# Gate weights' low half, table of further blocks and weight loads reordered at the entry into the experts of a hybrid decoder layer

## The chip, the core and the metric

The kernel runs on one core of a Trainium2 chip, in one launch. The metric is device time in microseconds. A core has five engines with queues of their own: PE (matmul; PEld is its weight load), DVE (vector), ACT (scalar), POOL (which here issues gathers and scatters) and SP (which here only issues loads). Sixteen DMA engines move the data for all of them.

## What is computed

One decoder layer over 1024 prompt tokens and 32 sample tokens, width 1024: an input projection, a convolution branch and a gated linear attention branch, an output projection, then a two-level mixture of experts, then a norm. The change lies where the experts begin.

```
g_idx  = argmax(softmax(x @ w_rg + b_rg))           # one of 4 groups
top_i  = top_k(e_logits of that group, 2)           # two of its 8 experts
# pairs (token, expert) sorted by expert, padded to blocks of 128 rows
xb = xt[row_tok].reshape(n_blocks, 128, D_MODEL)    # gather
hidden = silu(xblk @ w_g[e]) * (xblk @ w_u[e])      # 1024 -> 512
yb = hidden @ w_d[e]                                # 512 -> 1024
y = segment_sum(yb * row_wt, row_tok)               # scatter with add
```

## The kernel before

Tokens go through the layer in nine tiles of 128 (the last has 32). For each tile DVE picks group and experts and counts the rank of every pair inside its expert (`place`), then makes the pair's weight (`weigh`). Every expert has one block of 128 rows (blocks 0 to 31). Pairs beyond the 128th of an expert go to further blocks, at most 16, whose number is found at run time; in this run the trace shows 36 blocks in all. `lst_tok` (in the trace `kdT`) holds the tokens of each block, `lst_w` their weights. Both come out of bank 7, where PE adds one-hot products tile by tile; `list_last` adds the last tile, and DVE then copies the bank.

A block `n` is worked as follows, with two buffers for everything that has the index `n % 2`:

- SP loads three weight matrices of 2 MB each (`load_w`, L504: gate, up, down) into `wraw`, each when PE is done with the block before last in that buffer.
- POOL gathers the block's 128 token rows (`gather`, L988, `stage` in the trace, 4 KB a row).
- PE transposes them (`x_block`, L1524). ACT rounds them and the weights to a high half (`xeH`, `wH_`); DVE makes the low half, the rest (`x_low`, `weight_low`: `xeL`, `wL_`). A product is then three matmuls: high by high, high by low, low by high.
- PE does the gate product (24 matmuls of 512 columns), transposes the rows of block `n + 1`, does the up product (24) and the down product of block `n - 1` (24).
- POOL scatters the result with add into `h_scr` (`scatter`, L997), each scatter after the one before it has landed.

Every engine works through its own list in the order in which the code issues it; semaphores tie the lists together. `keep_running(n)` (L1107) is `n` matmuls of ones by the identity whose result nobody reads: it only keeps PE busy. Each of them shows in the trace as two records.

The steps at the entry, before the change, with their lines: DVE `weigh(8)` (L2613 to L2618), copy of the counts (L2740) and of `lst_w` (L2742), low half of the gate weights, `x_low(0)`, low half of the up weights, then the table of further blocks (L2749 to L2767, a dozen small operations on 16 partitions, which ends in `more_made`), then block 0. POOL: `gather(0)`, `gather(1)`, the last slots, `gather(2)`, then it waits for `more_made`, stores the table, gathers the further blocks' lists (`qe`), and goes on with `gather(3)`. SP: after `gather(0)` has landed, down weights of block 0, up weights of block 1, down weights of block 1.

## Time and profile before

| | us |
|---|---|
| time, median of 3 runs (1714.29 to 1717.73) | 1715.81 |
| the profiled execution's own time | 1714.82 |
| its span | 1713.0 |
| PE busy in the span | 1665.4 (97%) |
| DVE busy | 1264.9 (74%) |
| ACT busy | 930.4 (54%) |
| POOL busy | 248.8 (15%) |

The entry into the experts lies at about 1025 to 1050 us of the span, and the experts fill the time from there to about 1675 us. A busy share is a mean over stages with different limits, and a busy PE is not a PE at its peak. The profiled execution is one of many: its own time is 0.99 us under the median of the three.

### The profile page before, as it was taken

What the parts mean: (1) busy time and instruction counts of PE and PEld (TensorE: products, weight loads), DVE (VectorE), ACT (ScalarE), POOL (GpSimd) and SP (SyncE); (2) the same over time, 40 slices, a digit from 0 to 9 for tenths busy, and PEclk for the clock granted to TensorE, in tenths of its full rate; (3) what the DMA queues carried; (4) which work ended last, traced back from release to release, by engine and by line L of the source; (5) the groups of instructions that cost most, each with busy time, mean ns of one, the idle gap of its engine ahead of it and who ended that gap; (6) DMA issues with size and microseconds to landing.
All of it is one profiled execution on the core that took longest, in us unless ns stands there. A gap on an engine that the chain in (4) does not pass through costs nothing.

```text
span 1713.0 us, 24990 instructions
## 1 busy us (share of the span) xinstructions
PE 1665.4 (97%) x9010; PEld 1463.1 (85%) x9010; DVE 1264.9 (74%) x2101; ACT 930.4 (54%) x1184; POOL 248.8 (15%) x269
## 2 busy tenths in 40 slices
PE   8999999999999999999999999999999999999994
PEld 7999987777999999879998888888888888888882
DVE  5234799986766667655464558999889899889886
ACT  6363121216433344426343337887878778788785
POOL 4100111110000000011001123511111212122111
PEclk9999999999999999999999998999999999999998
DMA  5402223231243233366343339999999999999975
GB/s 203 145 26 75 75 100 107 94 108 57 93 142 105 93 93 93 102 199 214 117 166 129 105 105 373 390 394 380 383 378 384 377 382 371 377 381 381 384 276 221
DMA packets 103171, 367.26 MB, mean 214 GB/s; under 512 B 14628, under 2 KB 58872, under 8 KB 88240
## 3 DMA queue, kind: packets, MB, share of 16 engines
q1 hardware_dynamic: 79824, 308.76, 48.2%
q0 software_dynamic: 23056, 57.36, 10.3%
q8 instruction: 47, 0.77, 0.2%
q14 instruction: 36, 0.29, 0.1%
q10 hardware_dynamic: 208, 0.08, 0.0%
HBM read 326.24 MB, written 61.22 MB: 226 GB/s over the span
## 4 chain that ended last, share of the span: by engine, by line
PE 72%; PEld 15%; DMA 4%; DVE 3%; ACT 2%; issue 2%; DVEq 1%; SPq 0%; ACTq 0%; PEldq 0%; POOLq 0%
PE bank L1069 68%; PEld bank L1069 15%; PE bank L1524 2%; DMA wraw_down<-in_w_expert_down 1%; DMA wraw_up<-in_w_expert_up 1%; PE bank L1548 1%; DMA uo<-in_x_prompt 1%; DVE gwork L2107 1%; PE bank L1441 0%; DMA h_scr<-ybuf,kdT 0%; ACT L1641 0%; PEld bank L1288 0%; DMA s<-in_state_gla 0%; DMA wraw_gate<-h_scr 0%; DVE wraw_gate L2674 0%
## 5 line engine op out<-in xcount | busy, mean ns | idle before, releaser
L2107 DVE TENSOR_TENSOR wL_down<-wraw_down,wH_down 128x1024 fp32r<-128x1024 f32 x140 | 162.0, 1218 | 25.6 <-ACT wH_down L1641 25.1
L2107 DVE TENSOR_TENSOR wL_up<-wraw_up,wH_up 128x2048 fp32r<-128x2048 f32 x72 | 161.6, 2285 | 21.6 <-ACT wH_up L1641 21.6
L2107 DVE TENSOR_TENSOR wL_gate<-wraw_gate,wH_gate 128x2048 fp32r<-128x2048 f32 x72 | 161.7, 2287 | 12.1 <-ACT wH_gate L1641 12.1
L1641 ACT ACTIVATE wH_up<-wraw_up 128x2048 fp32r<-128x2048 f32 x72 | 134.0, 1909 | 66.2 <-DMA wraw_up<-in_w_expert_up 51.8
L2232 DVE SCALAR_TENSOR_TENSOR ybuf<-uo,gwork,ybuf 128x1024 f32<-128x1024 f32 x120 | 154.5, 1288 | 6.1 <-issue 6.1
L1641 ACT ACTIVATE wH_down<-wraw_down 128x1024 fp32r<-128x1024 f32 x140 | 136.6, 1051 | 18.5 <-DMA wraw_down<-in_w_expert_down 18.4
L1641 ACT ACTIVATE stage<-bank 128x512 f32<-128x512 f32 (+3 forms) x65 | 34.5, 546 | 190.2 <-PE bank L1069 180.8
L997 POOL DMA_INDIRECT h_scr<-ybuf,kdT x34 | 77.1, 2269 | 399.7 <-ACT ybuf L1641 360.9
L1641 ACT ACTIVATE wH_gate<-wraw_gate 128x2048 fp32r<-128x2048 f32 x72 | 134.5, 1934 | 1.2 <-DMA wraw_gate<-in_w_expert_gate 1.2
L1069 PE MATMUL bank<-nTH,gateH 128*128 128x352 f32 x384 | 129.5, 337 | 0.7 <-issue 0.6
L1069 PE MATMUL bank<-nTH,slabH 128*128 128x352 f32 x384 | 124.9, 325 | 1.2 <-ACT uo L1641 0.7
L1069 PE MATMUL bank<-nTH,gateL 128*128 128x352 f32 x384 | 124.0, 323 | 0.0
L1069 PE MATMUL bank<-nTL,gateH 128*128 128x352 f32 x384 | 123.5, 322 | 0.0
L1069 PE MATMUL bank<-nTH,slabL 128*128 128x352 f32 x384 | 123.2, 321 | 0.0
L1069 PE MATMUL bank<-nTL,slabH 128*128 128x352 f32 x384 | 123.1, 321 | 0.0
L1069 PE MATMUL bank<-wH_up,xeH 128*128 128x512 f32 x288 | 115.9, 403 | 0.0
L1069 PE MATMUL bank<-wH_gate,xeH 128*128 128x512 f32 x296 | 115.4, 390 | 0.0
L1069 PE MATMUL bank<-wH_gate,xeL 128*128 128x512 f32 x296 | 115.3, 390 | 0.0
L1069 PE MATMUL bank<-wH_up,xeL 128*128 128x512 f32 x288 | 112.7, 391 | 0.0
L1069 PE MATMUL bank<-wL_up,xeH 128*128 128x512 f32 x288 | 112.2, 390 | 0.0
L1069 PE MATMUL bank<-wL_gate,xeH 128*128 128x512 f32 x288 | 112.0, 389 | 0.0
L1069 PE MATMUL bank<-wH_down,hidTH 128*128 128x512 f32 x280 | 109.5, 391 | 1.2 <-DVE hidTL L2107 1.2
(359 smaller groups left out, 4279.5 us busy)
## 6 DMA issues: line engine op xcount, KB each, us to landing
wraw_gate<-in_w_expert_gate SPq DMA_DIRECT2D x36, 2048.0 KB, 19.1
wraw_up<-in_w_expert_up SPq DMA_DIRECT2D x36, 2048.0 KB
wraw_down<-in_w_expert_down SPq DMA_DIRECT2D x36, 2048.0 KB
slab_raw<-in_w_in SPq DMA_DIRECT2D x7, 2048.0 KB, 9.6
gate_scr<-stage POOLq DMA_DIRECT2D x16, 528.0 KB, 3.6
vr_scr<-stage POOLq DMA_DIRECT2D x32, 256.0 KB, 2.3
gate_raw<-in_w_in SPq DMA_DIRECT2D x16, 512.0 KB, 8.7
vrbuf<-vr_scr SPq DMA_DIRECT2D x16, 512.0 KB, 6.9
```

What stands on the lines that cost most here:

```text
L997: pool.indirect_dma_start(out=h_scr, in_=yo[n % 2], in_offset=None, out_offset=bass.IndirectOffsetOnAxis(ap=lst_tok[:, n:n + 1], axis=0), ...
L1069: return pe.matmul(out, lhsT=lhsT, rhs=rhs, start=start, stop=stop, **kw)
L1524: last = pe.transpose(bk[k // 4][:, P * (k % 4):P * (k % 4 + 1)], xg[b][:, k:D:KC], ident[:, :])
L1548: last = pe.transpose(bk[4][:, P * k:P * (k + 1)], hid[:, k:DE:FC], ident[:, :])
L1641: return act.activation(out, in_, func, **kw)
L2107: return dve.tensor_tensor(out, x, y, op)
L2232: dve.scalar_tensor_tensor(ybuf[:, c, 0:SEQ], u[:, c, bass.ds(w, SEQ)], tap, ybuf[:, c, 0:SEQ], ALU.mult, ALU.add)
```

## The change

On DVE, the gate weights' low half, `x_low(0)` and the up weights' low half come directly behind `weigh(8)`; the copies of the counts and of `lst_w` come after them, and the table of further blocks after block 2. On PE, four `keep_running` matmuls move from behind to ahead of the last list product of the tokens; sixteen instead of two stand ahead of `x_block(0)`; the last list product of the weights and the sum of the counts come behind it, and two instead of eight `keep_running` matmuls ahead of the first gate product. On POOL, `gather(3)`, `gather(4)` and `scatter(0)` come ahead of the wait for the table. On SP, the weight loads wait for `gather(0)` and `gather(1)`, and the up weights of block 1 come ahead of the down weights of block 0. The steps that follow the table move two blocks later, and PE and DVE run blocks 3, 4 and 5 written out, with the loop from block 6.

```diff
@@ SP
             sp.wait_ge(xg_loaded[0], 16)
+            sp.wait_ge(xg_loaded[1], 16)
+            load_w(sp, W_UP, 1, 1)
             load_w(sp, W_DOWN, 0, 0)
-            load_w(sp, W_UP, 1, 1)
             sp.wait_ge(hn_made, NT)
@@ POOL
             gather(2)
+            gather(3)
+            gather(4)
+            scatter(0)
             pool.wait_ge(more_made, 1)
...
-            for n in range(NE - 3):
+            for n in range(2, NE - 3):
                 gather(n + 3)
-                if n >= 1:
-                    scatter(n - 1)
+                scatter(n - 1)
@@ PE
             ranks(NT - 1)
+            keep_running(4, bk[3])
             pe.wait_ge(slot_made, 2 * NT - 1)
             list_last(tok_hot, 0).then_inc(tok_listed, 1)
-            keep_running(4, bk[3])
-            pe.wait_ge(w_hot_made, NT)
-            list_last(w_hot, NE).then_inc(w_listed, 1)
-            mm(bk[5][:, 0:NE], ones[:, 0:P], macc[:, :], True, True).then_inc(count_ready, 1)
...
             pe.wait_ge(lists_ready, 1)
+            keep_running(16, bk[3])
+            x_block(0, 16)
+            pe.wait_ge(w_hot_made, NT)
+            list_last(w_hot, NE).then_inc(w_listed, 1)
+            mm(bk[5][:, 0:NE], ones[:, 0:P], macc[:, :], True, True).then_inc(count_ready, 1)
             keep_running(2, bk[3])
-            x_block(0, 16)
-            keep_running(8, bk[3])
             block_products(0, 0, 16, None, first=True)
             block_products(1, 1, 32, None)
             block_products(2, 0, 32, None)
+            block_products(3, 1, 48, None)
+            block_products(4, 0, 48, None)
             pe.wait_ge(lists_f, 1)
...
-            block_products(3, 1, 48, None)
-            with pe.Fori(2, NE // 2 - 1) as i:
+            block_products(5, 1, 64, None)
+            with pe.Fori(3, NE // 2 - 1) as i:
@@ DVE
+            weight_low(W_GATE, 0, 0)
+            x_low(0, 0)
+            weight_low(W_UP, 0, 0)
             dve.wait_ge(count_ready, 1)
             dve.tensor_copy(cnt, bk[5][:, 0:NE])
             dve.wait_ge(w_listed, NT)
             dve.tensor_copy(by_turn(lst_w), in_turns(bk[7][:, NE:2 * NE]))
             dve.drain()
-            weight_low(W_GATE, 0, 0)
-            x_low(0, 0)
-            weight_low(W_UP, 0, 0)
+            dve_block(0, 0, True, None, first=True)
+            dve_block(1, 1, True, None)
+            dve_block(2, 0, True, None)
+
             dve.wait_ge(const_ready, 7)
...
             dve.tensor_copy(m_int, m_out).then_inc(more_made, 1)
-            dve_block(0, 0, True, None, first=True)
-            dve_block(1, 1, True, None)
+            dve_block(3, 1, True, None)
             dve.wait_ge(listed_rows, 16)
```

PE's list between the last rank product and the first gate product. In it `kdn,state` and `macc,ones` 32x32 are the rank product, `ebuf,kdT` a list product, `ident,ones` the `keep_running` matmuls, `ident,stage` the transposes of `x_block(0)`. Before:

```order
L1069 MATMUL bank<-kdn,state 32x32
L1069 MATMUL bank<-macc,ones 32x32
L1069 MATMUL bank<-ebuf,kdT 128x32 x2
L1069 MATMUL bank<-ident,ones 128x128 x4
L1069 MATMUL bank<-ebuf,kdT 128x32 x2
L1069 MATMUL bank<-macc,ones 128x32
L1069 MATMUL bank<-ident,ones 128x128 x2
L1524 MATMUL bank<-ident,stage 128x128 x8
L1069 MATMUL bank<-ident,ones 128x128 x8
L1069 MATMUL bank<-wH_gate,xeH 128x512
```

And now:

```order
L1072 MATMUL bank<-kdn,state 32x32
L1072 MATMUL bank<-macc,ones 32x32
L1072 MATMUL bank<-ident,ones 128x128 x4
L1072 MATMUL bank<-ebuf,kdT 128x32 x2
L1072 MATMUL bank<-ident,ones 128x128 x16
L1524 MATMUL bank<-ident,stage 128x128 x8
L1072 MATMUL bank<-ebuf,kdT 128x32 x2
L1072 MATMUL bank<-macc,ones 128x32
L1072 MATMUL bank<-ident,ones 128x128 x2
L1072 MATMUL bank<-wH_gate,xeH 128x512
```

The second list product and the sum of the counts have gone behind the transposes, and most of the idle matmuls ahead of them.

DVE's list from the end of `weigh(8)` (`ebuf<-kdn,pay`). `small<-bank` is the copy of the counts, `kdT<-bank` that of `lst_w`, `qe<-small,mtab` the first operation of the table. Before:

```order
L2618 TENSOR_SCALAR ebuf<-kdn,pay 32x32 x2
L2740 COPY small<-bank 128x32
L2742 COPY kdT<-bank 128x32
L2107 TENSOR_TENSOR wL_gate<-wraw_gate,wH_gate 128x2048 x2
L2107 TENSOR_TENSOR xeL<-bank,xeH 128x512 x2
L2107 TENSOR_TENSOR wL_up<-wraw_up,wH_up 128x2048 x2
L2107 TENSOR_TENSOR qe<-small,mtab 16x256
```

And now:

```order
L2623 TENSOR_SCALAR ebuf<-kdn,pay 32x32 x2
L2112 TENSOR_TENSOR wL_gate<-wraw_gate,wH_gate 128x2048 x2
L2112 TENSOR_TENSOR xeL<-bank,xeH 128x512 x2
L2112 TENSOR_TENSOR wL_up<-wraw_up,wH_up 128x2048 x2
L2748 COPY small<-bank 128x32
L2750 COPY kdT<-bank 128x32
L2112 TENSOR_TENSOR xeL<-bank,xeH 128x512 x2
```

The two copies stand behind the weights now, and block 0 (its `xeL` is the last row) follows without the table. The table now stands between the down weights of block 2 and the low half of its hidden rows.

POOL's list from the last slots of tile 7 (`slot_scr`) on. `stage` is a gather, `h_scr<-ybuf` a scatter, the three rows from `IOTA` on are what waits for the table. Before:

```order
L960 DMA slot_scr<-pay,small 36864x2 x4
L988 DMA stage<-xn_scr,kdT 128x1024 x2
L960 DMA slot_scr<-pay,small 36864x2 x2
L988 DMA stage<-xn_scr,kdT 128x1024
L1028 IOTA attn 128x32
L1030 DMA more_scr<-small 16x4
L1032 DMA qe<-slot_scr,small 16x256
L988 DMA stage<-xn_scr,kdT 128x1024 x2
L997 DMA h_scr<-ybuf,kdT 1056x1024
L988 DMA stage<-xn_scr,kdT 128x1024
```

And now:

```order
L961 DMA slot_scr<-pay,small 36864x2 x4
L989 DMA stage<-xn_scr,kdT 128x1024 x2
L961 DMA slot_scr<-pay,small 36864x2 x2
L989 DMA stage<-xn_scr,kdT 128x1024 x3
L998 DMA h_scr<-ybuf,kdT 1056x1024
L1032 IOTA attn 128x32
L1034 DMA more_scr<-small 16x4
L1036 DMA qe<-slot_scr,small 16x256
L989 DMA stage<-xn_scr,kdT 128x1024
L998 DMA h_scr<-ybuf,kdT 1056x1024
```

The gather behind the three rows was that of block 3 and is now that of block 5.

## Rows read from the trace of the kernel before

**Rows 1.** The page, part 2: DMA share in 40 slices of the span

```profile
DMA  5402223231243233366343339999999999999975
```

**Rows 2.** Stretches: length; PE, PEld, DVE, ACT, POOL busy; PE clock, DMA share, GB/s

```profile
1123.72:1141.47 17.75, 17.75 (x86) 14.90 (x85) 15.92 (x13) 14.45 (x15) 2.61 (x2) 1.00 1.02 404
1602.84:1620.59 17.75, 17.11 (x81) 14.06 (x80) 14.28 (x13) 14.03 (x15) 3.64 (x2) 1.00 1.01 390
```

**Rows 3.** Chain of waits by time (start us, us, what), 1095 to 1665

```profile
1114.74 0.90 PE bank L1524 x8
...
1132.49 0.90 PE bank L1524 x8
...
1588.01 23.36 DMA wraw_down<-in_w_expert_down
...
1636.74 22.68 DMA wraw_up<-in_w_expert_up
```

**Rows 4.** Gate loads, issue to landing, 1060 to 1110, then 1450 to 1640

```profile
DMA to landing us min/median/max: 11.4/11.4/11.4
...
DMA to landing us min/median/max: 21.3/22.3/24.3
```

**Rows 5.** Timeline of PE at the entry (start us, us, what)

```profile
1032.68 1.05 PE L1069 MATMUL bank<-ebuf,kdT 32*128 32x32 f32 x4 [1.64 <-DVEq L2608]
1033.66 2.08 PE L1069 MATMUL bank<-ident,ones 128*128 128x128 f32 x8
1038.21 1.97 PE L1524 MATMUL bank<-ident,stage 128*128 128x128 f32 x8
1039.97 3.21 PE L1069 MATMUL bank<-ident,ones 128*128 128x128 f32 x16
1042.93 0.48 PE L1069 MATMUL bank<-wH_gate,xeH 128*128 128x512 f32 x1
```

**Rows 6.** The same timeline, idle matmuls and a list product ten microseconds earlier

```profile
1021.99 2.03 PE L1069 MATMUL bank<-ident,ones 128*128 128x128 f32 x16
1027.21 0.66 PE L1069 MATMUL bank<-ebuf,kdT 128*128 128x64 f32 x4
```

**Rows 7.** Busy time in the two microseconds in which the granted clock changes

```profile
1032.00:1033.00 1.00, 0.32 (x2) 0.32 (x2) 0.70 (x5) 1.00 (x1) 0.00 (x0) 0.68 0.97 411
1042.00:1043.00 1.00, 1.00 (x9) 1.00 (x8) 1.00 (x3) 1.00 (x2) 1.00 (x1) 0.70 1.02 426
```

**Rows 8.** Timeline of DVE at the entry and in block 2, then one of ACT

```profile
1035.18 0.38 DVE L2618 TENSOR_SCALAR ebuf<-kdn,pay 32x32 f32<-32x32 f32 x2
1037.69 4.49 DVE L2107 TENSOR_TENSOR wL_gate<-wraw_gate,wH_gate 128x2048 fp32r<-128x2048 f32 x2
1042.10 1.28 DVE L2107 TENSOR_TENSOR xeL<-bank,xeH 128x512 fp32r<-128x512 f32 x2
1047.70 0.41 DVE L2107 TENSOR_TENSOR qe<-small,mtab 16x256 f32<-16x256 f32 x1
1050.99 0.16 DVE L2767 CAST small<-small 16x4 int32<-16x4 f32 x1
1093.42 4.61 DVE L2107 TENSOR_TENSOR wL_down<-wraw_down,wH_down 128x1024 fp32r<-128x1024 f32 x4
...
1039.42 0.60 ACT L1641 ACTIVATE xeH<-bank 128x512 fp32r<-128x512 f32 x1 [6.16 <-PE bank L1524]
```

**Rows 9.** Timeline of POOL at the entry

```profile
1034.88 1.07 POOL L988 DMA_INDIRECT stage<-xn_scr,kdT  x1 [3.95 <-DVE kdT L2637]
1036.25 1.03 POOL L988 DMA_INDIRECT stage<-xn_scr,kdT  x1 [0.30 <-issue]
1053.40 2.04 POOL L988 DMA_INDIRECT stage<-xn_scr,kdT  x1 [0.31 <-issue]
```

**Rows 10.** Gathers, issue to landing, 1045 to 1600; then the one of 1036.25

```profile
DMA to landing us min/median/max: 12.1/13.6/15.5
...
stage<-xn_scr,kdT POOLq DMA_INDIRECT x1, 4.2
```

More of the change, by code:

```diff
@@ L2774, in _ @@
             dve.tensor_copy(mlf[:, :, 1], mli[:, :, 1].bitcast(F32)).then_inc(lists_f, 1)
-            dve_block(2, 0, True, None)
+            dve_block(4, 0, True, None)
             dve.wait_ge(lists_T, 1)
@@ L2779, in _ @@
             dve.drain().then_inc(lists_ready, 1)
-            dve_block(3, 1, True, None)
-            with dve.Fori(2, NE // 2 - 1) as i:
+            dve_block(5, 1, True, None)
+            with dve.Fori(3, NE // 2 - 1) as i:
                 for b in range(2):
```

## The prediction

> **What bounds the kernel now.** I read four views, in this order. First the slices of the page: from the entry into the experts on, the DMA engines are busy in nine tenths or more of nearly every slice [rows 1]. A single block shows both limits side by side: PE busy 17.75 of 17.75 us and a DMA share of 1.02 [rows 2]. The transposes of two blocks follow each other at 1114.74 and 1132.49, so a block takes 17.75 us of PE [rows 3]. Second, the landing times say which of the two really has no room. A gate load takes 11.4 us from issue to landing early on and 22.3 us (21.3 to 24.3) late [rows 4]. The loads are issued by PE's progress, so landings that come ever later behind their issue mean that the DMA engines need a little more than 17.75 us for a block and fall back behind PE: by 22.3 - 11.4 = 10.9 us over some thirty blocks, about 0.36 us each. Third, the end of the chain of waits: it runs through a down load of 23.36 us (1588.01) and an up load of 22.68 us (1636.74) [rows 3], and just there PE is short of its full time for the first time (17.11 of 17.75, DMA share 1.01) [rows 2]. So PE sets the pace for most of the experts, and the DMA engines, which have caught up with its lead by about 1610, set the end. Fourth, the timelines at the entry, for the terms below.
>
> **The gate weights' low half.** DVE is through with `weigh(8)` at 1035.18 + 0.38 = 1035.56 and begins the gate weights at 1037.69 [rows 8], because it waits for a list product and the sum of the counts. It then needs until 1042.10, begins `x_low`, and PE's first gate product starts at 1042.93, 0.83 us behind that [rows 5, 8]. With the weights directly behind `weigh(8)` that is 2.13 us less, perhaps 0.1 of it lost to the handover: 2.0.
>
 The DVE way then gives a first gate product 2.0 + 0.4 = 2.4 us sooner, at 1040.5. The other way to it is the gather: issued at 1034.88, its rows were transposed from 1038.21, 3.33 us later [rows 5, 9]; now 1037.8. The sixteen idle matmuls ahead of it cost 32 records, twice the 2.03 us of 16 at the high clock [rows 6], 4.1 us from about 1033.6: 1037.7, just done. ACT's first half of `xeH` began 1.21 us after the transposes and took 0.60 [rows 5, 8]: 1039.6, no later than DVE's weights at 1039.7. The two list steps behind the transposes and the last two idle matmuls fit before 1040.5. So PE enters the experts 2.4 us sooner; if the clock does fall, see the third rival.
>
> **The wait of the weight loads.** They waited for the landing at 1038.2, at which the transposes start, and now wait for `gather(1)` too, which landed 4.2 us after 1036.25, at 1040.45, with the weights already running beside it [rows 9, 10]. Alone it should need the 3.33 us of the first: 1039.2 after the 0.4 us saved. So the loads start between 1039.2 and 1040.1, 1.0 to 1.9 us later. Against that, half of this gather's half megabyte has no more to be moved then; at the 404 GB/s of rows 2 that is 0.6 us. What the DMA engines begin later they end later, since they are never free again: a shift of 0.4 to 1.3 us, and I take 0.8. The exchange of up and down weights costs nothing: the three loads together are 6 MB, 16 us, and neither is used before PE has done a first up product.
>
> **The table moved.** It takes DVE from 1047.70 to 1050.99 + 0.16 = 1051.15, 3.45 us [rows 8]. It stood in the shadow of the first gate product; behind block 2 it stands in the stretch in which DVE works without a break, with its last down part ending at 1093.42 + 4.61 = 1098.03 [rows 8]. Less the 2.4 us of the entry that is 1095.6, or up to 1.9 later if the gate weights of block 2, the first to land behind the delayed loads, hold ACT up. The hidden rows of block 2 wait behind the table, until 1099.8 to 1101.6 with 0.7 for their own step; PE wants them behind the up product of block 3. The transposes ahead of that product stand a block before the 1114.74 of rows 3, at 1096.99, now 1094.6; they take 0.9, and the product a third of the rest of a block, about 5.5: near 1101.0. Cost: 0, at most 0.6.
>
> **What waits for the table.** This is the larger matter. POOL stands at the wait for `more_made` with `gather(5)` and `scatter(1)` behind it. The table is ready at 1095.6 + 3.45 = 1099.1 to 1101.0. Before, the gather behind it was issued 1053.40 - 1051.15 = 2.25 us after [rows 8, 9]; so `gather(5)` goes out between 1101.3 and 1103.2. Under the load of the weights a gather needs 13.6 us to land (12.1 to 15.5) [rows 10]: 1115.9, with bounds of 1113.4 and 1118.7. PE wants it in block 4, at 1114.74 - 2.4 = 1112.3 [rows 3]. So PE stands for 1.1 to 6.4 us, and I take 3.0, since less is queued ahead of it than late in the run. Nothing gives PE this back, but the DMA engines have 11.4 us of work queued at this time [rows 4], so they do not stand with it. `scatter(1)` is late too; it has until block 3's result is to be put into the same buffer, about 1124, some 20 us.
>
> What the Trainium skill says of this differs. "DMA: Bandwidth & Descriptors", section "Queues, rings and completion order", has each engine take turns between the queues that have work, a packet at a time. By that rule a gather beside the weights should need about twice its own time and not the time of all that is queued, and `gather(5)` would not stand in PE's way. The 12.1 to 15.5 us of rows 10 against 4.2 speak against it; the sum goes by the rows, and what would follow is in the first rival.
>
> **The sum.** On PE's way: -2.4 for the entry, +3.0 for `gather(5)`, 0 for the table: +0.6. On the DMA engines' way: +0.8. The end goes by the later of two ways that lie within a microsecond of each other, and by the end of the chain of waits by that of the DMA engines: +0.8 us. Against the profiled execution's own 1714.82 (span 1713.0 and 1.82 around it) this makes 1715.6; that execution is 0.99 under the median of the runs, so against the median of 1715.81 it is 1716.6.
>
> **Rivals.**
>
> 1. The entry's gain arrives whole. For it: PE is busy 97% of the span and sets each block's pace, and if gathers take turns with weights there is no stand in block 4. Against it: landings of 22 us late in the run [rows 4], and PE's first shortfall beside a DMA share of 1.01 [rows 2]. Time: 1715.8 - 2.4 = 1713.4, and that is still only 0.14%.
>
> 2. Slower: `gather(5)`, held by the table. If it is issued at 1103.2 and lands after 15.5 us, PE stands for 6.4 us; less 2.4 that is +4.0, and 1719.8. This decides when the stand is over 5.8 us, so that PE's way is over 3.4 us longer. For it: POOL's list, in which the gather stands right behind the wait. Against it: it needs late landings on both sides.
>
> 3. The clock falls all the same. Then the 32 idle records ahead of the transposes run at the low clock: eight of them took 2.08 us [rows 5], so 32 take some 8, from 1034 to 1042. From the start of the transposes to the end of ACT's first half 1.8 us passed [rows 5, 8], and from DVE's step to the first product 0.83: 1044.6, which is 1.7 us later than before. `gather(5)` is then wanted 4.1 us later than in the forecast and PE hardly stands for it. PE's way is +1.7 to +2.2. Time: 1715.8 + 1.9 = 1717.7. Against it: the idle matmuls now fill the stretch in which the clock fell.
>
> 4. The loads start 1.9 us late and each delay is kept, while PE stands little: 1717.1. This is the upper end of the forecast and not apart from it.
>
> **How the numbers follow.** Under 0.2%, 3.4 us, a measurement of this kernel cannot tell a change from none. Chances: forecast 0.60, gain kept 0.15, slower by the gather 0.13, clock falls 0.12. Faster by over 0.2% would need more than the whole 2.4 us of the entry: 0.07, most of it measurement. Slower by over 0.2%: most of the second rival and a part of the third: 0.16. Same: 0.77. The range runs from the first rival, 1713.3, to just short of the second, 1719.5.
>
> **What would show it.** After the change: the first gate matmul at 1040.5, with the granted clock at 1.00 throughout from 1030; SP's three loads at 1039.2 to 1040.1; DVE's table near 1096 to 1100; `gather(5)` issued at 1101 to 1103; an idle PE ahead of the transposes of block 5, near 1112; then, at the end, up and down loads of 20 us or more in the chain again, with the last up load landing at 1660 against 1659.4. The prediction is wrong if PE does not stand in block 4, if the last loads land as much earlier as PE is ahead (then the DMA engines did not set the end), or if the loss of the stand is carried to the end in full.

## The result, and the profile after

| | median us | runs |
|---|---|---|
| before | 1714.19 (1712.52 to 1718.98) | 20 |
| after | 1719.13 (1716.52 to 1723.98) | 20 |

The ratio is 1.0026, 95% interval 1.0018 to 1.0034: slower by over 0.2% in the middle of the interval. The profiled execution of the changed kernel took 1719.45 us, its span is 1717.5, against 1714.82 and 1713.0. Line numbers in the changed kernel are up to 5 higher for the helpers (L1072 was L1069, L2112 was L2107).

The page looks almost as it did [rows 1]. Three of the forty slices differ, by one digit each; one of them, lower, is at the entry:

```profile
DMA  5402223241243233356343338999999999999975
```

Two stretches of one block each (length; PE, PEld, DVE, ACT, POOL busy; PE clock, DMA share, GB/s):

```profile
1135.36:1153.11 17.75, 17.75 (x87) 14.90 (x86) 15.69 (x14) 14.44 (x15) 3.96 (x2) 1.00 1.01 385
1596.77:1614.52 17.75, 17.75 (x87) 14.90 (x86) 14.50 (x12) 13.02 (x14) 1.52 (x2) 1.00 1.01 379
```

PE is full in both, but the second is not the late stretch of [rows 2]: it ends where the transposes of block 33 start, and that of [rows 2] goes past them and takes in a wait that comes behind. The stretch from the transposes of block 33 to those of block 34 in the changed kernel, then in the kernel before, and there the one from block 34 to block 35 too:

```profile
1614.48:1635.09 20.61, 18.28 (x87) 14.74 (x86) 17.89 (x14) 17.42 (x17) 5.86 (x3) 1.00 0.96 367
```

```profile
1611.48:1630.15 18.67, 18.03 (x86) 14.81 (x85) 17.17 (x13) 15.83 (x16) 4.54 (x3) 1.00 0.95 358
1630.15:1648.72 18.57, 18.04 (x86) 14.82 (x85) 15.26 (x12) 16.21 (x16) 1.32 (x1) 1.00 0.99 366
```

So in both kernels the blocks take 17.75 us each up to block 33 and longer only at the very end.

**The entry.** PE's timeline, then DVE's, POOL's and SP's (start us, us, what), against [rows 5, 8, 9]:

```profile
1032.87 3.84 PE L1072 MATMUL bank<-ident,ones 128*128 128x128 f32 x32 [0.28 <-DVE kdT L2642]
1037.15 1.16 PE L1524 MATMUL bank<-ident,stage 128*128 128x128 f32 x8 [0.44 <-DMA stage<-xn_scr,kdT]
1039.65 0.50 PE L1072 MATMUL bank<-wH_gate,xeH 128*128 128x512 f32 x1
```

```profile
1034.50 4.49 DVE L2112 TENSOR_TENSOR wL_gate<-wraw_gate,wH_gate 128x2048 fp32r<-128x2048 f32 x2
```

```profile
1035.10 2.59 POOL L989 DMA_INDIRECT stage<-xn_scr,kdT  x1 [0.31 <-issue]
```

```profile
1040.86 0.33 SPq L504 DMA_DIRECT2D wraw_up<-in_w_expert_up  x1
1041.23 0.91 SPq L504 DMA_DIRECT2D wraw_down<-in_w_expert_down  x2
```

The first gate product starts at 1039.65 instead of 1042.93, 3.28 us sooner. The gate weights' low half starts 3.19 us sooner than the 1037.69 of before. The loads start at 1040.86, 2.68 us later than before (1038.18).

**Block 2.** ACT waits for the gate weights, and PE for their low half; three rows of ACT, DVE and PE, in this order:

```profile
1067.07 1.92 ACT L1646 ACTIVATE wH_gate<-wraw_gate 128x2048 fp32r<-128x2048 f32 x1 [5.46 <-DMA wraw_gate<-in_w_expert_gate]
...
1069.02 4.49 DVE L2112 TENSOR_TENSOR wL_gate<-wraw_gate,wH_gate 128x2048 fp32r<-128x2048 f32 x2 [4.35 <-ACT wH_gate L1646]
...
1071.46 0.47 PE L1072 MATMUL bank<-wH_gate,xeH 128*128 128x512 f32 x1 [1.95 <-DVE wL_gate L2112]
```

**The table and `gather(5)`.** DVE, POOL and PE, in this order:

```profile
1098.72 0.41 DVE L2112 TENSOR_TENSOR qe<-small,mtab 16x256 f32<-16x256 f32 x1
...
1102.08 0.67 DVE L2112 TENSOR_TENSOR hidTL<-bank,hidTH 128x512 fp32r<-128x512 f32 x1
```

```profile
1102.24 0.16 POOL L1032 IOTA attn<- 128x32 f32 x1 [22.20 <-DVE small L2776]
...
1104.45 2.62 POOL L989 DMA_INDIRECT stage<-xn_scr,kdT  x1 [0.31 <-issue]
```

```profile
1102.86 0.47 PE L1072 MATMUL bank<-wH_down,hidTH 128*128 128x512 f32 x1 [1.07 <-issue]
...
1116.95 1.16 PE L1524 MATMUL bank<-ident,stage 128*128 128x128 f32 x8 [2.46 <-DMA stage<-xn_scr,kdT]
```

POOL stood for 22.20 us at the table and then issued `gather(5)`. PE stood twice: 1.07 us ahead of the down product of block 2, and 2.46 ahead of the transposes of block 5. The profile puts the first down to "issue". It is the hidden rows' low half, which stood behind the table: DVE ends it at 1102.08 + 0.67 = 1102.75, and PE goes on at 1102.86. A product that needs several things at once can hide its last releaser in this way, and the timeline of the other engine tells it.

The chain of waits, as in [rows 3]: a chain through `gather(5)` first, then one block after the other, then the two loads.

```profile
1104.45 12.46 DMA stage<-xn_scr,kdT
...
1135.48 0.90 PE bank L1524 x8
1136.38 16.38 PE bank L1072 x72
1153.23 0.90 PE bank L1524 x8
...
1591.01 23.40 DMA wraw_down<-in_w_expert_down
...
1641.67 21.34 DMA wraw_up<-in_w_expert_up
```

The transposes give PE's place against before. At the start of block 5 they stand at 1116.95 instead of 1114.6 and from block 6 on 3.0 us behind (1135.36 by PE's timeline, 1132.3 before). They keep this distance for 28 blocks of 17.75 us. The late down load was issued 1591.01 - 1588.01 = 3.0 us later, the last up load landed at 1663.01 instead of 1659.42, 3.6 later, and the span is 4.5 longer. The way there, block by block, in us against before:

| block whose transposes start | 0 | 1 | 2 | 3 | 4 | 5 | 6 to 33 | 34 | 35 | end |
|---|---|---|---|---|---|---|---|---|---|---|
| after | -1.1 | -3.3 | -3.3 | -1.1 | -1.6 | +2.4 | +3.0 | +4.9 | +4.1 | +4.5 |

The gain of 3.3 us is there. 2.2 are lost to the late gate weights, 4.0 in block 4 (1.07 and 2.46 as above, and 0.5 that no wait shows). Two small differences of 0.5 and 0.6 lie where the loop starts, which is two blocks later, and cancel.

### The profile page after: what moved, and what is told of

Read it like the earlier page. It is cut to its first block, busy times and chain, and to the rows that moved or that the text cites. A ratio compares the mean times of both kernels' runs of the same rounds, so it can differ in the third digit from the quotient of the medians.

```text
span 1717.5 us, 24989 instructions
## 1 busy us (share of the span) xinstructions
PE 1667.1 (97%) x9026; PEld 1463.7 (85%) x9026; DVE 1264.8 (74%) x2101; ACT 930.9 (54%) x1184; POOL 236.8 (14%) x269
## 4 chain that ended last, share of the span: by engine, by line
PE 83%; DMA 6%; DVE 3%; issue 3%; ACT 2%; DVEq 1%; SPq 0%; ACTq 0%; POOL 0%; POOLq 0%
PE bank L1072 79%; DMA wraw_up<-in_w_expert_up 2%; PE bank L1524 2%; DMA wraw_down<-in_w_expert_down 1%; DMA stage<-xn_scr,kdT 1%; DMA uo<-in_x_prompt 1%; PE bank L1548 1%; DVE gwork L2112 1%; DMA h_scr<-ybuf,kdT 1%; PE bank L1444 0%; PE bank L1291 0%; ACT L1646 0%; ACT ybuf L1646 0%; DMA wraw_gate<-h_scr 0%; DVE wraw_gate L2679 0%
## 5 line engine op out<-in xcount | busy, mean ns | idle before, releaser
L2112 DVE TENSOR_TENSOR wL_up<-wraw_up,wH_up 128x2048 fp32r<-128x2048 f32 x72 | 161.6, 2285 | 23.7 <-ACT wH_up L1646 23.7
L2112 DVE TENSOR_TENSOR wL_down<-wraw_down,wH_down 128x1024 fp32r<-128x1024 f32 x140 | 162.0, 1219 | 22.7 <-ACT wH_down L1646 22.3
L2112 DVE TENSOR_TENSOR wL_gate<-wraw_gate,wH_gate 128x2048 fp32r<-128x2048 f32 x72 | 161.7, 2287 | 18.6 <-ACT wH_gate L1646 18.5
L1072 PE MATMUL bank<-nTH,gateH 128*128 128x352 f32 x384 | 129.5, 337 | 0.7 <-issue 0.6
L1072 PE MATMUL bank<-nTH,slabH 128*128 128x352 f32 x384 | 124.9, 325 | 1.2 <-ACT uo L1646 0.7
L1072 PE MATMUL bank<-nTH,gateL 128*128 128x352 f32 x384 | 124.0, 323 | 0.0
L1072 PE MATMUL bank<-nTL,gateH 128*128 128x352 f32 x384 | 123.5, 322 | 0.0
L1072 PE MATMUL bank<-nTH,slabL 128*128 128x352 f32 x384 | 123.1, 321 | 0.0
L1072 PE MATMUL bank<-nTL,slabH 128*128 128x352 f32 x384 | 123.1, 321 | 0.0
L998 POOL DMA_INDIRECT h_scr<-ybuf,kdT x34 | 67.3, 1980 | 401.8 <-ACT ybuf L1646 343.1
L1072 PE MATMUL bank<-wH_gate,xeH 128*128 128x512 f32 x296 | 115.5, 390 | 3.6 <-DVE wL_gate L2112 1.9
L1072 PE MATMUL bank<-wH_up,xeH 128*128 128x512 f32 x288 | 115.9, 402 | 0.0
L1072 PE MATMUL bank<-wH_gate,xeL 128*128 128x512 f32 x296 | 115.3, 390 | 0.0
L1072 PE MATMUL bank<-wH_up,xeL 128*128 128x512 f32 x288 | 112.7, 391 | 0.0
L1072 PE MATMUL bank<-wL_up,xeH 128*128 128x512 f32 x288 | 112.2, 390 | 0.0
L1072 PE MATMUL bank<-wL_gate,xeH 128*128 128x512 f32 x288 | 112.1, 389 | 0.0
L1072 PE MATMUL bank<-wH_down,hidTH 128*128 128x512 f32 x280 | 109.3, 391 | 1.7 <-issue 1.1
## 6 DMA issues: line engine op xcount, KB each, us to landing
wraw_down<-in_w_expert_down SPq DMA_DIRECT2D x36, 2048.0 KB, 19.5
```

Source lines behind the costliest of these rows:

```text
L998: pool.indirect_dma_start(out=h_scr, in_=yo[n % 2], in_offset=None, out_offset=bass.IndirectOffsetOnAxis(ap=lst_tok[:, n:n + 1], axis=0), ...
L1072: return pe.matmul(out, lhsT=lhsT, rhs=rhs, start=start, stop=stop, **kw)
L2112: return dve.tensor_tensor(out, x, y, op)
```

## The experiments

There are two theories, D and G where an expectation names them by a letter. D is the prediction's: the DMA engines, which are never free again, set the end, so the start of the loads counts and what PE loses is absorbed. G: PE's own way is carried to the end, and `gather(5)` is what the change costs. In every experiment the profile is one execution, and it lies up to 3.7 us from its kernel's median, so the verdict is the ratio's. It is against runs of before on the same chip. The three columns behind it are of the profiled execution: its own time, the start of the transposes of block 10 against the profile of before, and the span against that of before (1713.0).

| kernel | ratio (95% interval) | median us | profiled us | PE at block 10 | span |
|---|---|---|---|---|---|
| changed kernel | 1.0026 (1.0018 to 1.0034) | 1719.13 | 1719.45 | +3.0 | +4.5 |
| a_one_wait | 1.0025 (1.0014 to 1.0035) | 1718.14 | 1714.69 | +0.4 | -0.2 |
| a_gather5 | 1.0010 (1.0001 to 1.0019) | 1715.68 | 1717.72 | +2.0 | +2.9 |
| a_both | 1.0007 (0.9998 to 1.0016) | 1714.65 | 1712.41 | -1.8 | -2.4 |
| a_early_up | 1.0046 (1.0032 to 1.0061) | 1720.72 | 1719.96 | +5.7 | +5.1 |
| b_two_waits | 1.0002 (0.9993 to 1.0011) | 1714.97 | 1715.22 | +0.3 | +0.4 |
| b_entry | 1.0006 (0.9997 to 1.0015) | 1714.00 | 1714.00 | 0.0 | -0.9 |
| b_pe_late | 1.0027 (1.0018 to 1.0036) | 1717.65 | 1716.29 | +3.7 | +1.4 |
| b_early_up | 1.0030 (1.0019 to 1.0041) | 1719.46 | 1719.49 | +6.5 | +4.6 |
| c_entry_two_waits | 1.0004 (0.9995 to 1.0013) | 1715.25 | 1718.98 | +0.9 | +4.1 |
| c_entry_eight | 1.0004 (0.9995 to 1.0013) | 1714.66 | 1714.24 | 0.0 | -0.7 |
| c_both_eight | 1.0012 (1.0002 to 1.0022) | 1715.69 | 1714.19 | +0.5 | -0.7 |
| d_sent | 1.0006 (0.9997 to 1.0015) | 1715.03 | 1714.44 | +2.1 | -0.2 |

**One part of the change undone.** a_one_wait is the changed kernel without the wait for `gather(1)`:

```diff
             sp.wait_ge(xg_loaded[0], 16)
-            sp.wait_ge(xg_loaded[1], 16)
             load_w(sp, W_UP, 1, 1)
```

> The changed kernel, whose weight loads wait for the first gather alone, as before. Theory D (the start of the weight loads sets the end, since the DMA engines are never free again): the three loads start near 1037.2 instead of 1040.86, the gate weights of block 2 land some 3.5 us sooner than the 1067.05 of the changed kernel, and 3.5 of the 4.5 us in the span go away: ratio to the kernel before near 1.0005. Theory G (the stand for gather 5, behind the table, sets the end): PE still stands about 2.5 us in block 4; only the 1.9 us stand for the gate weights of block 2 goes: ratio near 1.0015.

a_gather5 has `gather(5)` ahead of the wait for the table, and a_both has both edits:

```diff
             gather(4)
             scatter(0)
+            gather(5)
             pool.wait_ge(more_made, 1)
...
             for n in range(2, NE - 3):
-                gather(n + 3)
+                if n > 2:
+                    gather(n + 3)
                 scatter(n - 1)
```

> The changed kernel, with the gather of block 5 ahead of POOL's wait for the table. Theory D: PE no longer stands in block 4 and is 2.5 to 4 us ahead through the middle of the experts, but loses it again in the last blocks, and the time is that of the changed kernel: ratio 1.0020 to 1.0026. Theory G: the 2.5 to 4 us stay gained to the end: ratio 1.0002 to 1.0010.

> The changed kernel with both: loads wait for the first gather alone, gather of block 5 ahead of the wait for the table. Theory D: as with the one wait alone, ratio 1.0000 to 1.0005 (loads about 1 us sooner than before at best: 0.9995). Theory G: the whole gain of the entry, 3 us, reaches the end: ratio 0.9982.

In a_one_wait the loads started 4 us sooner and the gate weights of block 2 came in time: PE was 4.2 us ahead of before at block 4. It then stood longer for `gather(5)`. Rows of SP, POOL and PE:

```profile
1036.90 0.33 SPq L504 DMA_DIRECT2D wraw_up<-in_w_expert_up  x1
...
1100.94 2.62 POOL L988 DMA_INDIRECT stage<-xn_scr,kdT  x1 [0.31 <-issue]
...
1114.37 1.16 PE L1523 MATMUL bank<-ident,stage 128*128 128x128 f32 x8 [3.38 <-DMA stage<-xn_scr,kdT]
```

1100.94 and 13.38 us to landing is 1114.32; whatever PE had gained before is gone there. The ratio stays at 1.0025, but the profile does not show where that comes from: its execution took 1714.69. The twelve executions of this kernel fall in two groups, five at 1714.4 to 1716.1 and seven at 1718.1 to 1724.9, and only one of the lower group was profiled. In a_gather5 `gather(5)` goes out 22 us sooner than in the changed kernel and PE does not stand for it, though it still stands for the table. POOL, then PE:

```profile
1081.99 1.37 POOL L989 DMA_INDIRECT stage<-xn_scr,kdT  x1 [0.30 <-issue]
...
1104.51 0.47 PE L1074 MATMUL bank<-wH_down,hidTH 128*128 128x512 f32 x1 [1.06 <-issue]
```

The ratio falls from 1.0026 to 1.0010, some 2.7 us. From block 4 to block 5 PE loses 1.3 us against before in this profile and 4.0 in that of the changed kernel, again 2.7, and the stand for the gather was 2.46. A second pair on one chip says the same: a_both differs from a_one_wait by this edit alone, and its median is 3.5 us lower. So the larger part of the loss is the held gather, and D, which expected 1.0020 to 1.0026 of a_gather5, lies just outside its interval. a_both should have been faster than before by G and was not shown to be, 1.0007. Its profiled execution was: PE stayed 1.8 us ahead and the time was 1712.41, third of eleven.

**The other parts alone, on the kernel before.** b_two_waits has only SP's change (both waits, up weights of block 1 first). b_entry has only the PE and DVE change at the entry, with the table where it was. b_pe_late makes PE late, with 16 more idle matmuls:

```diff
             x_block(0, 16)
-            keep_running(8, bk[3])
+            keep_running(24, bk[3])
             block_products(0, 0, 16, None, first=True)
```

> The kernel before with nothing but the changed order and wait of the weight loads. Theory D: the loads start 2 to 3 us later and the end moves by as much: ratio 1.0012 to 1.0018. Theory G: neither table nor gather 5 is touched, PE has room in blocks 1 and 2, ratio 1.0000 to 1.0004.

> The kernel before with nothing but the entry on PE and DVE: gate and up low halves behind the last weighing, the idle matmuls and list products as in the change; the table stays ahead of block 0, the loads wait for the first gather alone. Theory D (start of the weight loads sets the end): PE is 3 us ahead through the middle, the loads start about 1 us sooner because the first gather does, and the end moves by -1 us or not at all: ratio 0.9994 to 1.0000. Theory G (PE's own way sets the end, the change lost by the stand for gather 5): the 3 us reach the end: ratio 0.9982.

> The kernel before with 16 more idle matmuls ahead of the first gate product (24 instead of 8), so that PE enters block 0 about 3.7 us later at full clock while loads and gathers start as before. Theory D: PE is 3 to 4 us behind through the middle, the DMA engines catch up with it that much less, PE stands less in the last blocks, and the end moves by 0 to 2 us: ratio 1.0000 to 1.0010. Theory G (PE's way): the end moves by the whole 3.7 us: ratio 1.0022.

SP in b_two_waits, then PE in b_pe_late, then the two last stretches of b_pe_late from transposes to transposes (columns as above):

```profile
1041.14 0.33 SPq L504 DMA_DIRECT2D wraw_up<-in_w_expert_up  x1
```

```profile
1040.47 6.38 PE L1069 MATMUL bank<-ident,ones 128*128 128x128 f32 x48
1046.60 0.48 PE L1069 MATMUL bank<-wH_gate,xeH 128*128 128x512 f32 x1
```

```profile
1615.14:1632.88 17.74, 17.74 (x86) 14.89 (x85) 15.28 (x13) 14.91 (x15) 4.19 (x3) 1.00 1.00 369
1632.88:1650.63 17.75, 17.75 (x86) 14.90 (x85) 15.46 (x12) 15.49 (x16) 0.47 (x2) 1.00 1.01 376
```

Loads 3 us later, PE as before: 1.0002. PE 3.7 us later (1046.60 against 1042.93), loads as before: 1.0027, or 4.6 us (3.1 to 6.2). This pair speaks against D, which expected 1.0012 to 1.0018 for the late loads and at most 1.0010 for the late PE. The profile of b_pe_late also shows what is true of D. PE's transposes are 3.7 us late up to block 33 and 1.9 late at block 35, and the span is 1.4 longer: the late PE does not wait there, where the PE of before took 18.67 and 18.57 us. So at the end the loads have caught up with PE, and an earlier PE waits for up to the 1.7 us that those two stretches take over 17.75. Why the median of this kernel does not show that part is open; the profiled execution was its second fastest of ten. b_entry has the first gate product at 1040.60, and is at 1.0006 all the same. Its rows of POOL, SP and PE say where the 2.3 us went:

```profile
1035.54 2.59 POOL L988 DMA_INDIRECT stage<-xn_scr,kdT  x1 [0.30 <-issue]
...
1037.71 0.33 SPq L504 DMA_DIRECT2D wraw_down<-in_w_expert_down  x1
...
1048.39 1.16 PE L1521 MATMUL bank<-ident,stage 128*128 128x128 f32 x8 [2.09 <-DMA stage<-xn_scr,kdT]
```

`gather(1)` landed 12.81 us after its issue (1048.35), not 4.2 as in [rows 10], and PE stood for 2.09 us. POOL was through with issuing it at 1038.13, after the first load had gone out at 1037.71. The second wait of the change keeps the loads from doing this: in the four profiles with it and the new entry the gather took 5.7 to 5.9 us.

**Loads earlier.** a_early_up (on a_gather5) and b_early_up (on before) load the up weights of block 1 directly behind the gate weights, with no wait:

```diff
             load_w(sp, W_GATE, 1, 1)
+            load_w(sp, W_UP, 1, 1)
             sp.wait_ge(xg_loaded[0], 16)
```

> The changed kernel with the gather of block 5 ahead of the wait for the table, and with the up weights of block 1 loaded directly behind the gate weights of block 1, with no wait; only the down weights wait for the first gather. The engines for DMA then have no pause between 1035 and 1040. Theory D: 2 MB, some 5 us, are moved in a pause; the first gather lands 1 to 3 us later; the end moves by -2 to -4 us: ratio 0.9977 to 0.9990. Theory G: PE enters 1 to 3 us later than in the changed kernel and does not stand in block 4: ratio 0.9985 to 0.9995, by PE's way alone.

> The kernel before with the up weights of block 1 loaded directly behind the gate weights of block 1, with no wait; nothing else. Theory D: the end moves by -2 to -4 us although PE enters block 0 no sooner, or even 1 to 3 us later: ratio 0.9977 to 0.9990. Theory G: PE enters 1 to 3 us later because the first gather lands later, and the end moves by as much: ratio 1.0006 to 1.0018.

PE's transposes of block 0, in a_early_up and then in b_early_up:

```profile
1043.11 1.94 PE L1525 MATMUL bank<-ident,stage 128*128 128x128 f32 x8 [4.54 <-DMA stage<-xn_scr,kdT]
```

```profile
1043.97 1.97 PE L1524 MATMUL bank<-ident,stage 128*128 128x128 f32 x8 [6.38 <-DMA stage<-xn_scr,kdT]
```

Earlier loads slow the gather (9.0 and 9.8 us from issue to landing instead of 3.3), PE stands for it, and the time goes up by 5 to 8 us. Had the start of the loads set the end, both kernels would have gained.

**Why the entry's gain doesn't reach the median.** c_entry_two_waits is b_entry with SP's change, that is, the change without the move of the table. c_entry_eight has in it eight instead of sixteen idle matmuls ahead of `x_block(0)`, c_both_eight the same in a_both:

```diff
             pe.wait_ge(lists_ready, 1)
-            keep_running(16, bk[3])
+            keep_running(8, bk[3])
             x_block(0, 16)
```

> The entry change on PE and DVE and the changed wait and order of SP's loads, with the table where it was before (behind the up weights' low half of block 0), so that gather(3), gather(4) and gather(5) go out as before. Theory that PE's own way sets the end: first gate product at 1040 to 1041 against 1042.9, gather(1) lands near 1041 and PE does not stand ahead of the transposes of block 1 (it stood 2.1 us there with one wait), and nothing holds gather(5). If the gain stays, PE is 2 to 3 us ahead at block 10 and the ratio is 0.9982 to 0.9990. Rival: the loads begin later, the gate weights of block 2 land as late as in the changed kernel (1067, 2.2 us of PE lost), the gain is gone by block 3 and the ratio is 0.9998 to 1.0006.

> As the kernel with the entry change and two waits, but keep_running(8) instead of keep_running(16) ahead of the transposes of block 0. Theory that the 32 idle records run past the landing of gather(0) in typical executions (6.6 and 5.2 us at the low clock in two profiles, transposes at 1038.9 instead of 1037.2): ratio 0.001 lower than that kernel. Rival, they only fill a wait: ratio the same within 0.0007, or higher, if PE idles and the clock is at 1.2 GHz when the first gate products start.

> The changed kernel without the wait for gather(1), with gather(5) ahead of the wait for the table, and keep_running(8) instead of keep_running(16) ahead of the transposes of block 0. With sixteen the ratio was 1.0007 [0.9998, 1.0016]. Theory that the idle records at the low clock eat the entry's gain: 0.9990 to 0.9998. Rival, what is lost is the landing of gathers beside the weights: 1.0003 to 1.0010.

c_entry_two_waits has the rival's ratio, 1.0004, and c_entry_eight the same. Their profiles show five things that take from the gain, each in some executions only. First, the granted clock. PE rows of c_entry_two_waits, then of c_both_eight, then one stretch of each (columns as above):

```profile
1034.10 5.63 PE L1070 MATMUL bank<-ident,ones 128*128 128x128 f32 x32 [0.28 <-DVE kdT L2638]
1039.56 1.05 PE L1522 MATMUL bank<-ident,stage 128*128 128x128 f32 x8
```

```profile
1037.89 1.17 PE L1525 MATMUL bank<-ident,stage 128*128 128x128 f32 x8 [2.44 <-DMA stage<-xn_scr,kdT]
...
1048.96 1.05 PE L1525 MATMUL bank<-ident,stage 128*128 128x128 f32 x8
```

```profile
1032.00:1036.00 4.00, 3.72 (x17) 3.36 (x17) 1.64 (x12) 0.90 (x1) 1.04 (x1) 0.50 0.36 144
```

```profile
1041.00:1045.00 4.00, 4.00 (x12) 3.23 (x12) 3.38 (x2) 3.67 (x3) 3.51 (x2) 0.50 1.01 425
```

In c_entry_two_waits ACT begins them 1.4 us later still (1068.49 against 1067.07), and no stand of PE is recorded: it had lost its lead a block earlier, by the next thing.

Third, the table in its old place, ahead of block 0. Rows of c_entry_two_waits, DVE and then PE:

```profile
1051.23 0.16 DVE L2768 CAST small<-small 16x4 int32<-16x4 f32 x1
...
1054.93 0.47 PE L1070 MATMUL bank<-wH_gate,xeH 128*128 128x512 f32 x1 [1.04 <-DVE wL_gate L2108]
```

DVE ends the table at 1051.39, does `x_low` and begins the gate weights of block 1 only at 1052.51, and a PE that is ahead stands for them; from the transposes of block 1 to those of block 2 it takes 13.57 us instead of 12.29. With the table behind block 2, in the changed kernel, it takes 12.29. Fourth, `gather(1)` where there is one wait, as in b_entry. Fifth, the end of the experts: in c_entry_two_waits PE is 0.9 us late at block 10 and 3.1 late at block 34, since five of the blocks from 26 on take 17.8 to 19.5 us, and its span is 4.1 longer. This is its slowest execution of eleven. So the gain stated for c_entry_two_waits was not there: the rival's ratio came, but not by the rival's way, since not the gate weights of block 2 but those of block 1, behind the table, took most of what was lost by block 3. Eight idle matmuls instead of sixteen brought nothing in either kernel (1.0004 against 1.0004, 1.0012 against 1.0007), which speaks against the theory that the idle records alone eat the gain. How often each of the five takes it in the executions without a profile stays open.

d_sent was to make the fourth safe without the late loads: the loads wait for `gather(0)` and for POOL to be through with issuing `gather(1)`, on a_both:

```diff
             gather(1)
+            pool.drain().then_inc(const_ready, 1)
...
             sp.wait_ge(xg_loaded[0], 16)
+            sp.wait_ge(const_ready, 8)
```

> The changed kernel with gather(5) ahead of the wait for the table, and SP's loads waiting for gather(0) to land and for POOL to be through with issuing gather(1), not for gather(1) to land. In the profiles with one wait, gather(1) landed 5.9 and 6.1 us behind its issue where POOL was through with it before the first load (1036.5 against 1036.9, 1037.3 against 1037.3) and 12.8 and 11.8 us where a load was 0.4 us ahead (1038.1 against 1037.7, 1038.2 against 1037.9). Theory that this race takes the entry's gain in typical executions of the kernel with one wait (ratio 1.0007): the loads now start near 1037.7, gather(1) lands after about 6 us in every execution, PE is 2 to 2.5 us ahead at block 10, ratio 0.9985 to 0.9995. Rival: the median's loss lies elsewhere (the clock during the idle matmuls, late weights), ratio 1.0003 to 1.0010.

It did not do what it was meant to. POOL and SP:

```profile
1035.35 2.58 POOL L989 DMA_INDIRECT stage<-xn_scr,kdT  x1 [0.31 <-issue]
1043.36 2.99 POOL L961 DMA_INDIRECT slot_scr<-pay,small  x1 [5.42 <-issue]
```

```profile
1042.64 0.33 SPq L504 DMA_DIRECT2D wraw_up<-in_w_expert_up  x1
```

The drain let POOL go on only near 1042.6, 4.7 us after the issue ended, and everything behind it was late: PE, 3.0 us ahead at block 1, was 2.1 behind at block 10. The theory that the race of loads and `gather(1)` takes the gain is untested by it. Its ratio, 1.0006, goes with loads that start 4.5 us later than before (1042.64 against 1038.18).

**Taken together.** The ratios stand in two groups. With `gather(5)` held by the table: 1.0026 and 1.0025. With it free: 1.0010, 1.0007, 1.0012, 1.0006, and with the table in its old place 1.0002, 1.0006, 1.0004, 1.0004. Outside the two groups stand the three kernels that make PE start late, b_pe_late and the two with early loads: 1.0027, 1.0030 and 1.0046. No version was shown to be faster than the kernel before: the best are level with it.

## Why the prediction was right or wrong

The measured 1719.13 lies in the range (1713.3 to 1719.5) but 2.5 us over the forecast, and "slower" had only 0.16. That it lies inside is partly luck. The forecast of +0.8 us was added to a median of three runs, 1715.81, and that of twenty is 1714.19. The change itself costs 4.5 us by the ratio (3.1 to 5.8) and 4.9 by the medians, several times the forecast, and the range reached only 3.7 above its base. The mechanisms were named, and the account of what sets the end was wrong.

- **What sets the end: failed.** "Nothing gives PE this back, but the DMA engines have 11.4 us of work queued at this time [rows 4], so they do not stand with it", and with it "The end goes by ... that of the DMA engines: +0.8 us". The prediction read landings that come ever later behind their issue as DMA engines that fall behind PE. b_pe_late and b_two_waits show the reverse: PE later by 3.7 us costs 1.0027, loads later by 3 us are not seen to cost anything (1.0002, 0.9993 to 1.0011). The landing times of 22 us are those of a backlog that PE did not have to wait for: from block 6 to block 33 it needs 17.75 us for each, in every profile but that of c_entry_two_waits. What holds of the account is the end of it: from block 33 to block 35 the kernel before took 1.7 us more than two times 17.75, and b_pe_late nothing more. So the DMA engines could absorb 1.7 us of PE's loss, and the prediction let them absorb all of it. Its own test ("wrong if the loss of the stand is carried to the end in full") came out against it: +3.0 for 28 blocks.
- **The entry: right, and under-sized.** 2.4 forecast, 3.28 measured (at 1039.65, forecast 1040.5). The weights' low half came 3.19 sooner, since `weigh(8)` ended 1.1 sooner (1034.42 against 1035.56), not 0.4. The list product ahead of it took 0.63 us instead of 1.05, which is the forecast 0.4 (though its 0.66 in [rows 6] was read from a product of another shape), and it began 0.7 sooner, which the sum did not have. The clock was full where it counts, as a stretch of the changed kernel shows (columns as above), though it had been low just before:

```profile
1026.00:1030.00 4.00, 3.68 (x29) 3.60 (x30) 2.46 (x18) 1.26 (x6) 3.08 (x4) 0.59 1.03 436
1030.00:1040.00 10.00, 9.27 (x73) 8.34 (x72) 8.51 (x26) 5.23 (x5) 6.11 (x4) 0.99 0.49 186
```

  That was not sure: in c_entry_two_waits, with the same idle matmuls, it was at 0.50 from 1032 to 1036, which is the prediction's third rival.
- **The wait of the loads: 1.0 to 1.9 forecast, 2.68 measured.** `gather(1)` was issued over 2.59 instead of 1.03 us and took 5.7 to land. The prediction asked what late gate weights of block 2 do to DVE ("up to 1.9 later") and not what they do to PE. That is the missing term: 2.2 us.
- **The table: 0, at most 0.6 forecast, 1.07 measured.** The way was as described (hidden rows behind the table), and its start at 1098.72 inside the 1096 to 1100 named. With the gate weights in time it costs next to nothing: this wait is 0.2 us in a_one_wait and absent in a_both.
- **`gather(5)`: right in its way and size.** Issue forecast at 1101.3 to 1103.2, measured 1104.45; flight 13.6, measured 12.46; stand 1.1 to 6.4 and taken 3.0, measured 2.46. Moving it alone gives back 2.7 us in the ratio. The page of the Trainium skill that was weighed there, "DMA: Bandwidth & Descriptors" (section "Queues, rings and completion order"), says that queues take turns packet by packet. The prediction read this as twice a gather's own time, by which there would be no stand, and took the slow landings for evidence against the page. The 12.46 us speak against that reading only: a count of packets in b_entry, in the last section, shows turns being taken, in packets of very different size.
- **The sum.** With PE's way as the end, the terms as forecast give +0.6. As measured they give -3.3 + 2.2 + 1.1 + 2.5 = +2.5, which with 0.5 unassigned in block 4 is the +3.0 of the profile. The median's +4.9 is 1.9 more. The profile has 1.5 of this behind block 33: from its transposes to those of block 34 it took 20.61 us instead of 18.67, with an idle PE for 1.66 ahead of a gate product at 1629.09, which the profile puts down to "issue". What it waited for was not settled.
- **The rivals.** The second named the right mechanism and made it decide only when the stand is over 5.8 us. That threshold came from the wrong account of the end. The first (gain kept whole) did not come without the table's move either, in c_entry_two_waits and b_entry.

## What to carry to other kernels

Before an engine that is 97% busy is called absorbed by a queue, ask whether the queue's work is issued by that engine's own progress: then its growing landing times are no proof that it sets the end. A kernel in which the engine alone is late (b_pe_late) tests it in one run, if both are read: the ratio, and at which block of the profile the lateness shrinks. When a step is moved behind later work, list what stands behind its consumer in every in-order queue: here a gather that had nothing to do with the table stood behind POOL's wait for it, and cost more than the table. A gain at the head of a pipeline is kept only if each next transfer is ahead too; here gate weights, table, gathers and clock each took a part of it. And a profile of one execution explains a median only where its own time is near it.

## What the runs showed of the hardware that was not expected

- **POOL's issue of a gather takes 2.58 to 2.59 us instead of 1.03 when DVE has begun the weights' low half before it.** The issue of `gather(1)` took 1.03 in the four kernels with the old entry and 2.58 or 2.59 in all ten with the new one, where `wL_gate` (two steps of 2.25 us, both inputs in SBUF) had started 0.6 us before. It ended 0.94 us behind the first of the two steps (1034.50 + 2.25 = 1036.75; 1037.69). The Trainium skill, "SBUF — State Buffer", section "SBUF: two separate sides", says that DVE with two SBUF inputs and a GpSimd operation that reads SBUF lock each other out for a whole instruction, and the one that came first keeps the ports. The trace agrees as far as POOL goes: `gather(1)` came second and was longer, and `gather(0)`, begun 0.77 us before `wL_gate`, took its 1.07 as ever. It does not show DVE held: the first step of `wL_gate` began while `gather(0)` was still being issued and took 2.29 us, as the same step does at 1048.84.
- **A race of 0.4 us decides over some 6 us of a gather's flight.** With one wait, `gather(1)` landed after 5.9 and 6.1 us where POOL had ended its issue at 1036.52 and 1037.29 and the first load went out at 1036.90 and 1037.28. It took 12.8 and 11.8 us where the issue ended at 1038.13 and 1038.22 and the load went out at 1037.71 and 1037.87. The queue rows of b_entry from 1041 to 1047 (packets, MB, share of the engines) show how, q1 being the loads and q0 the gathers and slots:

```profile
q1 hardware_dynamic: 153, 2.24, 88.1%
q0 software_dynamic: 147, 0.30, 12.9%
```

  Both queues are served at the same time, nearly packet for packet, but a packet of the loads holds some 15 KB on average and one of q0 some 2. So the gather gets an eighth of the bytes, and not a half.
- **A drain on POOL behind a gather held it for 4.7 us** (d_sent), from 1037.93 to 1042.64. The gathers' queue moved its last packets between 1040 and 1041, so the drain is no cheap mark for "issued".
